# A two-layer block: the last attention's scores and the differential attention's product with the values moved to split fp32r, and several waits rearranged

## What is computed

```python
# second model, layer 0: differential attention, 8 heads of 2 x 64, 512 latent + 256 context queries
s = jnp.einsum('bqhmd,bkhmd->bhmqk', qb, keys).astype(f32) * ATTN_SCALE
p = jax.nn.softmax(s, axis=-1)
a = p[:, :, 0] - lam * p[:, :, 1]
o = jnp.einsum('bhqk,bkhe->bqhe', a.astype(vals.dtype), vals)
o = rms_norm_2(o, subln_g, SUBLN_EPS) * (1.0 - lam_init)      # then * silu(g), and @ w_o[0]
# second model, layer 1: windowed attention, 16 heads of 64, 4 key heads, a learned sink per head
s_band = jnp.einsum('bqhgd,bjhd->bhgqj', qb, kb).astype(f32) * ATTN_SCALE
s_ctx = jnp.einsum('bqhgd,bjhd->bhgqj', qb, kc).astype(f32) * ATTN_SCALE
p = sink_softmax(jnp.concatenate([s_ctx, s_band], axis=-1)).astype(vb.dtype)
ox = p[..., :n_ctx] @ vc + p[..., n_ctx:] @ vb                # written short
# around each: x = x + gate * (o @ w_o[i]), with rms_norm_2 and a modulation ahead of the projections
```

## Time and profile before

| | |
|---|---|
| median of 3 runs | 1648.8 us (1647.83 to 1648.9) |
| time of the profiled execution | 1646.68 us |
| its span, from the first to the last instruction | 1644.8 us |
| PE busy | 1563.3 us (95%) |
| PE's weight loads busy | 1216.7 us (74%) |
| DVE busy | 976.7 us (59%) |
| ACT busy | 752.2 us (46%) |
| POOL busy | 507.1 us (31%) |
| mean granted clock of PE | 0.982 |
| share of the chain that ended last: L337 | 39% |
| the same: L341 | 19% |

### The profile page before, as it was taken

The page is one execution under the profiler, slowest core; times in us unless marked ns, Lnnn a source line. Parts: engine busy times, 40 slices in busy tenths (PEclk is TensorE's granted clock), DMA queues, the critical chain, the costliest instruction groups (busy, mean ns, idle before and its releaser), DMA issues.

```text
span 1644.8 us, 23387 instructions
## 1 busy us (share of the span) xinstructions
PE 1563.3 (95%) x8248; PEld 1216.7 (74%) x8248; DVE 976.7 (59%) x2254; ACT 752.2 (46%) x1413; POOL 507.1 (31%) x233
## 2 busy tenths in 40 slices
PE   7998999999899999999899999999999889999997
PEld 5886666678688888888787787777877668865566
DVE  6236555365689857646656766667574366157742
ACT  6225766634342314243334455445553432257753
POOL 3651332345244444444121111122124533320012
PEclk9999999999999999999799999999999989999998
DMA  6861122363365665633111111111111122210001
GB/s 199 177 154 33 59 66 70 110 230 128 103 206 188 196 196 186 202 117 92 37 52 50 41 39 39 38 38 40 37 39 54 49 67 77 83 58 1 1 21 57
DMA packets 48400, 149.33 MB, mean 91 GB/s; under 512 B 5782, under 2 KB 9110, under 8 KB 48184
## 3 DMA queue, kind: packets, MB, share of 16 engines
q1 hardware_dynamic: 37080, 112.45, 22.9%
q10 hardware_dynamic: 11232, 35.72, 6.7%
HBM read 141.53 MB, written 6.62 MB: 90 GB/s over the span
## 4 chain that ended last, share of the span: by engine, by line
PE 77%; DVE 9%; issue 5%; ACT 5%; POOL 2%; DMA 1%; ACTq 0%; POOLq 0%; DVEq 0%; SPq 0%
PE ps L337 39%; PE ps L341 19%; PE ps L538 3%; PE ps L557 3%; PE ps L568 3%; PE ps L1321 3%; PE ps L1285 2%; DVE b_sb L662 2%; POOL w_l L950 1%; PE ps L1297 1%; ACT sb L623 1%; PE ps L405 1%; PE ps L1050 1%; ACT w_h L322 1%; DVE b_sb L697 1%
## 5 line engine op out<-in xcount | busy, mean ns | idle before, releaser
L950 POOL TENSOR_TENSOR w_l<-raw,w_h 128x1024 fp32r<-128x1024 f32 (+1 forms) x190 | 457.4, 2409 | 905.7 <-ACT w_h L322 886.0
L322 ACT ACTIVATE w_h<-raw 128x1024 fp32r<-128x1024 f32 x190 | 200.6, 1057 | 376.2 <-PE ps L337 317.0
L337 PE MATMUL ps<-x2h,w_h 128*128 128x512 f32 (+1 forms) x816 | 245.8, 366 | 23.7 <-DVE x2l L1971 9.1
L337 PE MATMUL ps<-x1h,w_h 128*128 128x512 f32 x584 | 237.1, 406 | 16.0 <-POOL w_l L950 10.4
L341 PE MATMUL ps<-x2l,w_h 128*128 128x512 f32 (+1 forms) x816 | 231.8, 349 | 0.0
L337 PE MATMUL ps<-x2h,w_l 128*128 128x512 f32 (+1 forms) x816 | 231.5, 349 | 0.0
L337 PE MATMUL ps<-x1h,w_l 128*128 128x512 f32 x584 | 230.0, 394 | 0.0
L341 PE MATMUL ps<-x1l,w_h 128*128 128x512 f32 x584 | 229.3, 393 | 0.0
L337 PEld LDWEIGHTS ps<-x2h,w_h 128*128 128x128 f32 x816 | 132.2, 191 | 57.4 <-issue 20.1
L337 PEld LDWEIGHTS ps<-x2h,w_l 128*128 128x128 f32 x816 | 132.3, 191 | 21.0
L341 PEld LDWEIGHTS ps<-x2l,w_h 128*128 128x128 f32 x816 | 132.9, 191 | 19.6
(11 more groups left out here) (305 smaller groups left out, 2583.2 us busy)
## 6 DMA issues: line engine op xcount, KB each, us to landing
raw<-in_w_mlp SPq DMA_DIRECT2D x64, 512.0 KB, 3.7
mraw<-in_w_mod ACTq DMA_DIRECT2D x51, 512.0 KB, 3.7
raw<-in_w_a SPq DMA_DIRECT2D x32, 512.0 KB, 3.6
raw<-in_w_att SPq DMA_DIRECT2D x25, 512.0 KB, 11.8
raw<-in_w_b SPq DMA_DIRECT2D x20, 512.0 KB, 3.6
raw<-in_w_g SPq DMA_DIRECT2D x16, 512.0 KB, 3.7
raw<-in_w_ao SPq DMA_DIRECT2D x9, 512.0 KB, 3.6
gates<-g_stage ACTq DMA_DIRECT2D x16, 256.0 KB, 2.3
```

The lines of the kernel that those rows point to most:

```text
L322: nc.scalar.activation(split(u)[0], raw[:, u % RAW], ACT.Copy).then_inc(w_hi, 1)
L337: mm = nc.tensor.matmul(o, w[:, k], xh(k), start=(first and k == k0 and wi == 0), stop=(last and k == k1 - 1 and wi == 1))
L950: nc.gpsimd.tensor_tensor(l[:, ks], raw[:, u % RAW, ks], h[:, ks].bitcast(F32), ALU.subtract).then_inc(w_lo, 1)
```

## The change

In the differential heads the product with the values is made of fp32r parts, for two query blocks at a time: ACT's copy of the transposed weights (`a_pth`) becomes the high part, DVE makes the low part (`turned_low`), and the values get a high and a low part (`a_vh`, `a_vl`). `weigh(n)` multiplies three forms for 256 columns. ACT now does `turned` ahead of the exponentials. In the last attention the scores are three fp32r forms in place of one float32 form; the queries and keys get high and low parts when they are rotated. In the same attention the low part of a finished group is made a step later, between the two halves of the minima. The output tiles of layer 0 are multiplied latent columns first, then context columns, with only five of eight squares added on POOL. The context squares are taken between the shifts, and the context tiles' modulation moves from units 3 to 6 to units 4 to 7. At the very end DVE adds a square one tile earlier. The diff, cut to what the text speaks of:

```diff
@@ scores of both attentions: one form, or three
                 for c in range(nk):
-                    for h in range(2):
-                        o, rhs = st["k"](h)[c]
-                        mm = nc.tensor.matmul(A.sbank(m + h)[:, o:o + rhs.shape[-1]], st["q"](r + h), rhs,
-                                              start=st["kstart"][c], stop=True, skip_group_check=True)
+                    for x, (qx, kx) in enumerate(st["forms"]):
+                        for h in range(2):
+                            o, rhs = st[kx](h)[c]
+                            mm = nc.tensor.matmul(A.sbank(m + h)[:, o:o + rhs.shape[-1]], st[qx](r + h), rhs,
+                                                  start=(x == 0), stop=(x == last), skip_group_check=True)
...
+                                        forms=[("q", "k"), ("ql", "k"), ("q", "kl")], off=C, keys=C + n, rp=rp, bias=lambda j, mask=mask: mask,
@@ DVE in the last attention
             for n in range(n0, len(A.steps)):
                 if n + 1 < len(A.steps):
-                    attn_minima(v, A, n + 1)
+                    attn_minima(v, A, n + 1, (0, 1))
+                finished(n - 3, "low")
+                if n + 1 < len(A.steps):
+                    attn_minima(v, A, n + 1, (2, 3))
                 attn_scale(v, A, n)
-                if n >= 2:
-                    finished(n - 2)
+                finished(n - 2)
                 A.between_dve(v, n)
...
+        def fin2_low(v, A, n, g):
+            h, l, gg, tmp = A.steps[n]["dst"]
             v.wait_ge(A.k2, g + 1)
             nc.vector.tensor_tensor(l, tmp, h.bitcast(F32), ALU.subtract).then_inc(A.ol, 1)
@@ POOL after the heads
-            add_squares(nm4, N_OUT - 1, 0, S)
+            add_squares(nm4, SQ_ADDED, 0, S)
+            low(U_B)
             low(U_B + 1)
@@ PE, last_out
-                for m in range(N_OUT):
-                    pe.wait_ge(wo_free[1], m + 1)
...
+                for n in range(2 * N_OUT):
+                    m = n % N_OUT
+                    cols = slice(0, S) if n < N_OUT else slice(S, SC)
+                    out = ps[:, 2 + n % 4, 0:cols.stop - cols.start]
+                    if n >= 4:
+                        pe.wait_ge(wo_free[1], n - 1)
...
-                nm4.wait(pe, "add", N_OUT - 2)
+                nm4.wait(pe, "add", SQ_ADDED - 1)
                 column_sums(sqsum, 6, S, True, False)
-                nm4.wait(pe, "sq", N_OUT)
-                column_sums(sq[:, 1], 6, S, False, True).then_inc(nm4.mm, 1)
+                for m in range(SQ_ADDED, N_OUT):
+                    nm4.wait(pe, "sq", m + 1)
+                    mm = column_sums(sq4[m], 6, S, False, m == N_OUT - 1)
+                mm.then_inc(nm4.mm, 1)
@@ PE, a differential head
                 def turns(qt):
                     wait_head(pe, "a", head, 6, qt + 1)
                     if qt == 0:
-                        wait_head(pe, "ve", head, 1, 1)
+                        wait_head(pe, "vl", head, 1, 1)
                     else:
-                        wait_head(pe, "te", head, 6, qt)
+                        wait_head(pe, "tl", head, 6, qt)
...
+                def weigh(n):
+                    wait_head(pe, "tl", head, 6, 2 * n + 2)
+                    blocks = range(6) if n < 2 else range(4, 6)
+                    for y, b in enumerate(blocks):
+                        for x, (v, p) in enumerate(((a_vh, a_pth), (a_vh, a_ptl), (a_vl, a_pth))):
+                            mm = nc.tensor.matmul(ps[:, 3 + 2 * n, C:2 * C], v[:, b, :], p[:, y, :], start=(x == 0 and y == 0),
+                                                  stop=(x == 2 and y == len(blocks) - 1))
+                    mm.then_inc(ha["pv"], 1)
...
                 for qt in range(4):
                     scores(qt + 2)
                     dense(2 if more else 4 + (qt == 0))
+                    if qt == 2:
+                        weigh(0)
                     turns(qt)
                     dense(1 + qt % 2 if more else 3)
+                dense(2)
+                weigh(1)
                 turns(4)
-                dense(4)
-                wait_head(pe, "m", head, 12, 12)
-                wait_head(pe, "te", head, 6, 4)
-                for b in range(6):
-                    mm = nc.tensor.matmul(ps[:, 6], a_v[:, b, :], a_pt[:, b, :], start=(b == 0), stop=(b == 5))
-                if not more:
-                    dense(3)
+                dense(2 if more else 4)
                 turns(5)
-                if more:
-                    dense(4)
-                wait_head(pe, "te", head, 6, 6)
-                for b in range(2):
-                    mm = nc.tensor.matmul(ps[:, 7, 0:C], a_v[:, 4 + b, :], a_pt2[:, b, :], start=(b == 0), stop=(b == 1))
-                mm.then_inc(ha["pv"], 1)
-                dense(4 if more else 7)
+                dense(4 if more else 3)
+                weigh(2)
+                dense(4 if more else 5)
@@ ACT, a differential head
                 def turned(qt):
                     wait_head(act, "t", head, 6, qt + 1)
+                    if qt >= 2:
+                        wait_head(act, "pv", head, 3, qt // 2)
...
                 for qt in range(6):
+                    if qt == 5 and more:
+                        take((i, c + 1), 2, True)
+                    turned(qt)
                     if qt < 4:
                         exps(qt + 2, 0)
                         if qt == 2 and more:
                             take((i, c + 1), 1, True)
                         exps(qt + 2, 1)
-                    if qt == 5 and more:
-                        take((i, c + 1), 2, True)
-                    turned(qt)
@@ DVE, a differential head
+                def turned_low(qt):
+                    n = 6 if qt < QT else 2
+                    wait_head(v, "te", head, 6, qt + 1)
+                    cols = slice(qt % 2 * P, (qt % 2 + 1) * P)
+                    nc.vector.tensor_tensor(a_ptl[:, 0:n, cols], pair(2)[:, 0:n * P].rearrange("p (b q) -> p b q", b=n),
+                                            a_pth[:, 0:n, cols].bitcast(F32), ALU.subtract).then_inc(ha["tl"], 1)
...
+                wait_head(v, "ve", head, 1, 1)
+                nc.vector.tensor_tensor(a_vl[:].rearrange("p b e -> p (b e)"), pair(2)[:, 0:SC],
+                                        a_vh[:].rearrange("p b e -> p (b e)").bitcast(F32), ALU.subtract).then_inc(ha["vl"], 1)
                 for qt in range(6):
                     combine(qt)
                     if qt == 0 and c > 0 and more:
                         output((i, c - 1))
+                    if qt:
+                        turned_low(qt - 1)
                     if qt < 4:
                         mins(qt + 2)
                 if more:
                     rotate((i, c + 1), 0, "q")
                     rotate((i, c + 1), 1, "k")
+                turned_low(5)
                 gated(head)
@@ ACT, the last layer's units
             def take_b(u):
+                if 4 <= u < 4 + KT // 2:
+                    for k in (2 * (u - 4), 2 * (u - 4) + 1):
+                        nm4c.wait(act, "t", k + 1)
+                        shift_tile(k, 1, xn2, 1).then_inc(nm4c.hi, 1)
                 unit_done(act, U_B + u)
                 split_high(act, U_B + u + 2)
...
-                    if 3 <= u < 3 + KT // 2:
-                        for k in (2 * (u - 3), 2 * (u - 3) + 1):
-                            nm4c.wait(act, "t", k + 1)
-                            shift_tile(k, 1, xn2, 1).then_inc(nm4c.hi, 1)
@@ DVE, the last layer's units
-                if 3 <= u < 3 + KT // 2:
+                if 4 <= u < 4 + KT // 2:
...
+                    for k in (2 * (u - 4), 2 * (u - 4) + 1):
+                        nm4c.wait(v, "hi", k + 1)
+                        low_tile(k, 1, xn2, 1).then_inc(nm4c.lo, 1)
...
-                    done(nc.vector.tensor_tensor(x, ropeb[:, 1, :], ropeb[:, 2, :], ALU.add))
+                    done(nc.vector.tensor_tensor(ropeb[:, 0, :], ropeb[:, 1, :], ropeb[:, 2, :], ALU.add))
                     settle(v)
...
+                    if u < 8:
+                        done(nc.vector.tensor_copy(b_qh[:, u, :], ropeb[:, 0, :]))
+                        settle(v)
+                        done(nc.vector.tensor_tensor(b_ql[u], ropeb[:, 0, :].rearrange("p (a q) -> p a q", a=2),
+                                                     b_qh[:, u, :].bitcast(F32).rearrange("p (a q) -> p a q", a=2),
+                                                     ALU.subtract))
+                        settle(v)
@@ DVE, the end
-                if j:
-                    add_square(v, nm5, j - 1, S)
+                if j < KT - 1:
+                    add_square(v, nm5, j, S)
```

More of the change, by code:

```diff
@@ L430, in build @@
         nm3b = Norm(add=0, mm=0)
-        nm4 = Norm(src=0, add=N_OUT - 2)
+        nm4 = Norm(src=0, add=SQ_ADDED - 1)
         nm4c = Norm(src=0, add=KT - 1)
         nm5 = Norm(src=0, add=KT - 1, r=2, t=FIN, hi=0, lo=0)
```

(19 more changed lines are left out.)

124 lines of the change are left out of this document (68 added, 56 removed).

## The result

The changed kernel takes 1706.45 us (median of 4 runs, 1705.33 to 1709.13) against 1648.3 us for the kernel before on the same chip: a ratio of 1.0357, 95% interval 1.0344 to 1.0370. It is slower, as forecast with 0.84, but the time lies 17.9 us over the 1688.6 forecast and 6.5 over the range's upper end. The profiled execution took 1709.13 us, its span 1707.0 us, 62.2 more than the span before.

A forecast was written before the change was run, and what follows sets the result against it. PE's work was taken as the bound, unless PE is made to wait. Heads +35.0, clock +16.0, output and query units +3.5, attention -14.0, end -0.7 gave +39.8: 1686.5 us profiled, median 1688.6, range 1656 to 1700.

The forecast's parts named there:

- `weigh(2)` behind the rotations: Head's end: PE waits 5.9 us at `weigh(2)` for DVE's last low part, queued behind both rotations until +12.55.
- The loss is 2.3 us, of which I take 2.0: Heads: the pause brings the 1.2 GHz level, costing 2.0 us a head, 14.0 over seven heads, or nothing.
- one head's sum: Differential heads: 6.41 + 18.5 - 19.89 = +5.0 us a head, +35.0 over seven; clock counted separately.
- split, copy and rotation bring DVE to 1354.0: Query units: after unit 3 at 1347.5, DVE is ready at 1354.0, then three turns to 1377.7.
- The turn of 7.9 us: Query units: tiles, shift, split, copy and rotation run serially, about 7.9 us a turn against PE's 5.44.
- 5.3 us earlier until unit 3: Output tiles and query units: earlier sums, the ended 2.77 us wait and small waits bring 5.3 us, bounds 2.8 to 6.
- 1.24 a pair: Last attention: 32 score pairs take 39.7 us; new forms 0.82 to 0.98, about 0.28 less each, 8.8 in all.
- Faster: Rival: DVE's rotations do not hold up `weigh(2)`, PE waiting under 2.5 us a head; -17.8, 1631 us; chance 0.12.
- The clock stays up: Rival: the wait in the heads is there but the clock holds; +23.8, 1672.6 us; chance 0.20.
- no collision: Rival: POOL's work misses DVE's rotations in the heads and the clock holds; +9.8, 1658.6 us; chance 0.14.
- its rival's 5: Rival: the last attention gives only 5 us, its idle time taken by the next wait; 1697.6 us; chance 0.08.
- The loads: Rival: weight loads slow each fp32r product in the heads to 0.28 us; +54, some 1743 us; chance 0.02.

The follow-up runs named there:

- experiment 1: Changed kernel with DVE making the low part for block 5 between the two rotations instead of behind both: 1665.23 us, ratio 1.0108.
- experiment 3: Changed kernel with the differential heads of the kernel before, all else as changed: 1647.59 us, ratio 1.0004.
- experiment 5: Changed kernel, next queries' rotation ahead of block 4's low part, block 5's low part in the middle of the keys' rotation: 1659.14 us, ratio 1.0066.
- Experiment 9: Changed kernel with DVE's head-end list rearranged, context tiles ahead of rotations, and DVE's heads 1 to 6 written out instead of looped: 1634.21 us, ratio 0.9925.
- experiment 4: Changed kernel with context tiles' modulation back beside units 3 to 6 in the old order, rotations keeping their low parts: 1706.98 us, ratio 1.0353.
- experiment 8: Kernel before plus the last attention's part alone (three-form scores, rotations' low parts, group's low part a step later): 1654.26 us, ratio 1.0035.
- experiment 6: Changed kernel with the heads of before, DVE taking the inverse and all context tiles ahead of unit 2's rotation: 1632.06 us, ratio 0.9909.
- experiments 11 and 12: Experiment 6 with the group's low part back in its old place: 1637.06 us; experiment 6 with the last attention's scores in float32: 1633.50 us.
- experiment 2: Changed kernel with 18 unread fp32r products on PE just ahead of the third product with the values: 1691.57 us, ratio 1.0262.
- experiment 10: Experiment 9 with PE's last two value-unit steps ahead of the second product with the values, both low parts mid keys' rotation: 1647.23 us, ratio 0.9994.

## Why the prediction went wrong, point by point

**Right.** The sign, the mechanism and its place: `weigh(2)` behind the rotations, shown by experiments 1 and 3. The products with the values run 0.119 us apart (18 in 2.15 us in experiment 5), and the loads are hidden. DVE was done as forecast (+12.5); the wait was put at 5.9 us and is 4.6, because PE comes later: 0.77 us that I had counted as nothing stand ahead of it. The value unit's end no longer lies under a product with the values, and PE waits for ACT's copy. The sum of both, 5.3, is near.

**The clock: near.** A fall behind each pause was forecast, with 2.0 us a head ("The loss is 2.3 us, of which I take 2.0"). 2.2 a head came back when the pause was filled; the length of the lower stretch, taken from one place in the earlier trace rows, differs between heads by a factor of two. The rest of the 20 us lies behind the waits of the next point.

**The heads: the step that failed** is one head's sum, with its clock 7.0 us, times seven. In five heads it holds, at 7.1, with a wait too long and a clock loss too small, which is partly luck. In the two at which DVE's loop starts again the loss is 11.3 a head, 22.6 and not 14.0: 5.1 us of waits for minima, and the lower clock behind them. The jump back is in no term of the prediction. Experiment 9 shows it: without it seven heads are 7.8 us shorter.

**Query units: the step that failed** is "split, copy and rotation bring DVE to 1354.0". It took DVE as free when unit 3 is copied. Set back by the 59.3 us by which the last head's scores start later, DVE came to the tiles at 1359.3. Its queue had grown from unit 0 on: three rotations at 6.4 us, which I had put at 4.9 with their low parts, since each holds an operation stretched by POOL, now to 2.5 or 2.8 us where I had 1.61; and the inverse behind them, with 5.1 us on PE that I did not have at all. That wait also made unit 4 late, so that DVE, done with the first two tiles, stood 4.1 us for its copy (1420.57 to 1424.63). The 5.3 us from 1354.0 to 1359.3 and these 4.1 are most of the 10.5 by which the stretch was mis-sized (16.0 us, not 5.5). The turn of 7.9 us was right (8.07), but naming the serial order as the cause was not: experiment 4 undoes it and gains nothing, experiment 8 has the loss without it, and experiment 6 gets all back by order alone.

Two smaller errors stand in the same paragraph. "5.3 us earlier until unit 3" came out as 1.6 (ACT copies that unit at 1410.76, less 59.3 that is 1351.5, and 1353.12 before): the 2.77 us wait is gone and the sums start 3.1 us earlier (2 forecast), but PE now sums two squares more itself, so that the next product starts 11.4 us behind the sums' start (1381.61) and not 7.8, and the clock stays at the lower level there for 17 us instead of 10. And 1379.5 less 1375.78 is 3.7, where the sum used 3.5.

**The last attention: a term mis-sized.** "1.24 a pair" was busy time divided by pairs, which holds each group's way through the array. From start to start they took 1.17 us on average and now 1.02: 5.0 us and not 8.8 (the middle of the "0.82 to 0.98" for the new form would even have made it 10.9). The idle time gave 4.6, where I had 5.2. And their shares were the other way round: experiments 11 and 12 give 6.3 us to the move of the low part and 3.0 to the forms.

**The rivals.** "Faster" decided from 2.5 us of waiting, with 12.0 us from the rest. In experiment 1 PE waits 1.7 us in a head and the kernel is 1% slower: the rest is worth nothing (experiment 3), so its bound was wrong too. "The clock stays up" is refuted, and so is "no collision" (3.03 us). The last attention gave 9.9 us, between its rival's 5 and the 14.0. The loads are not in the way.

**The sum.** 39.8 forecast, 62.2 found: heads +9.3, sums to unit 8 +10.5, the last attention +4.1, the start +1.0, the rest -2.5.

## What to carry to other kernels

Before adding work to an engine with idle time, write down its queue in order with what each item waits for: here one 0.42 us operation cost 41 us by standing behind 11 us of rotations that nobody needed yet, and in the query units a 0.17 us reciprocal stood behind 19. Put first what the bound engine waits for, and move the rest behind it. A pause of some us on PE can cost twice, once in waiting and again in clock. The parts of such a change are worth trying apart: the version with the old heads and the tiles first beats both kernels, and it keeps all of the change but the heads. And a loop that grows is worth a look at its restarts: writing this one out for one engine gave 7.8 us.

## What the runs showed of the hardware

**A jump back on DVE** cost 2.2 to 2.4 us in the changed kernel: DVE stands still that long at both restarts of a loop that holds two heads, 86 DVE operations each; with 79 each, before and in experiment 3, 0.17 us. DVE's first operation for the minima at a restart, changed and before:

```profile
1029.07 0.06 DVE L2186 MEMSET small<- 128x1 f32 x1 [2.22 <-issue]
```

```profile
1004.57 0.95 DVE L2161 CUSTOM_DVE_ANT_0 a_p<-ps,small 128x768 f32<-128x768 f32 x1 [0.17 <-issue]
```

The view of DMA shows code being fetched there. Queues of the changed kernel over 1026:1034, around the first restart:

```profile
q1 hardware_dynamic: 144, 0.52, 19.6%
q14 instruction: 3, 0.02, 1.1%
```

Three packets of the instruction queue q14 lie there, and three more over 1149:1157, around the second. Before, none of q14 lies between 960 and 1210, through both restarts. Over the whole kernel q14 carried 35 packets before, 45 in the changed kernel, and 37 with DVE's loop written out (experiment 9), where DVE doesn't stand still. So with the longer body DVE's code is fetched again at the restart, and DVE waits for it. A longer loop without the new work was not tried, and no run shows from what length on it happens.

**DVE and POOL.** While POOL subtracts a weight's low part (2.4 to 2.6 us), a DVE operation that starts meanwhile can take 1.8 to 3.0 us instead of 0.4 to 1.0, and ends when POOL's does or up to 0.8 us later. Not all are: a STREAM_SHUFFLE at 1395.23 took its usual 0.75. The Trainium skill ("GPSIMD Engine Reference", 1. Specifications) speaks of contention with DVE instructions in a 2-port mode or with two SBUF inputs. The trace agrees for the subtraction, which has two (0.96 us, 3.03 with POOL). A rounding, with one input, was drawn out as well (0.43 us, 2.50 at 1405.31); whether it ran in a 2-port mode no view shows.

**The clock and short pauses.** Bare pauses of 4.5 to 4.6 us in dense work brought the 1.2 GHz level each time, and 1.4 us in experiment 1 never. Between them length alone does not decide: 2.39 and 2.70 us in the changed kernel brought it, 2.46 us in experiment 2 and 2.77 us before did not, and in experiment 10 pauses of 1.84 to 1.97 us did in three heads of seven, the longest not among them.
